# Five products per weight tile in place of six in a two-layer encoder step, with a reduction on VectorE at each evacuation

## The reference, cut to what matters

```
h = rms_norm(x, norm_ffn_w)
gate, val = split(h @ w_up)                 # 1024 -> 2 x 2816
conv = conv_b + sum_j shift(gate, j) * conv_w[j]      # width 3
x = x + (gelu(conv) * val) @ w_down         # 2816 -> 1024
```

## Time and profile before

| | |
|---|---|
| median of 3 runs | 1358.85 us (1358.19 to 1364.44) |
| span of the profiled execution | 1358.6 us |
| TensorE matmul busy | 1270.3 us, 93% |
| VectorE busy | 831.5 us, 61% |
| GpSimd busy | 688.2 us, 51% |
| ScalarE busy | 252.1 us, 19% |

### The profile page before, as it was taken

One profiled execution on the slowest core, in us unless ns is written; L12 is line 12 of the kernel. 1 busy time (PEld: TensorE's weight loads), 2 busy tenths in 40 slices (PEclk: granted clock), 3 DMA queues, 4 the chain that ended last, 5 costly groups with the idle time before them and its releaser, 6 DMA issues.

```text
span 1358.6 us, 24821 instructions
## 1 busy us (share of the span) xinstructions
PE 1270.3 (93%) x9637; PEld 1222.5 (90%) x9637; DVE 831.5 (61%) x1271; ACT 252.1 (19%) x502; POOL 688.2 (51%) x562
## 2 busy tenths in 40 slices
PE   5989999999999999999999987689999999999995
PEld 4977699999999999999999875379999999999995
DVE  7986577877778742228214556746877778772113
ACT  3023331121111210012111113523121111210000
POOL 5541155665655656665543332025755656655660
PEclk9989999999999999999999889999999999999998
DMA  5220112222222223332241110021332232222221
GB/s 200 77 86 17 33 63 94 80 90 88 82 93 80 90 78 99 99 120 80 78 126 59 52 47 32 0 73 63 94 93 78 92 93 77 93 78 93 93 77 67
DMA packets 34948, 108.91 MB, mean 80 GB/s; under 512 B 5920, under 2 KB 7728, under 8 KB 34896
## 3 DMA queue, kind: packets, MB, share of 16 engines
q1 hardware_dynamic: 28656, 102.51, 23.5%
q10 hardware_dynamic: 6240, 5.64, 1.3%
HBM read 103.00 MB, written 5.13 MB: 80 GB/s over the span
## 4 chain that ended last, share of the span: by engine, by line
PE 44%; DVE 34%; issue 13%; ACT 7%; DVEq 2%; DMA 0%; ACTq 0%; SPq 0%
PE psum L376 13%; PE psum L377 12%; PE psum L378 12%; DVE conv L1128 8%; DVE sq L1142 4%; DVE conv L1133 3%; DVE conv L1130 3%; ACT conv L779 2%; DVE gate L1081 2%; ACT y_hi L784 2%; DVE rstd L1074 1%; PE psum L504 1%; DVE sumsq L1060 1%; DVE even_winsum L1217 1%; PE psum L524 1%
## 5 line engine op out<-in xcount | busy, mean ns | idle before, releaser
L376 PE MATMUL psum<-h_hi,w_hi 128*128 128x272 f32 x2096 | 617.4, 295 | 25.6 <-DVE h_lo L1069 16.9
L378 PE MATMUL psum<-h_hi,w_lo 128*128 128x272 f32 x2096 | 611.9, 292 | 0.0
L377 PE MATMUL psum<-h_lo,w_hi 128*128 128x272 f32 x2096 | 609.0, 291 | 0.0
L354 POOL TENSOR_TENSOR w_lo<-w_raw,w_hi 128x1024 fp32r<-128x1024 f32 x187 | 461.6, 2469 | 15.6
L376 PEld LDWEIGHTS psum<-h_hi,w_hi 128*128 128x128 f32 x2096 | 400.2, 191 | 30.0 <-issue 12.6
L377 PEld LDWEIGHTS psum<-h_lo,w_hi 128*128 128x128 f32 x2096 | 401.0, 191 | 0.3
L378 PEld LDWEIGHTS psum<-h_hi,w_lo 128*128 128x128 f32 x2096 | 400.0, 191 | 0.0
L351 POOL TENSOR_TENSOR tick<-tick 1x1 f32<-1x1 f32 x183 | 36.8, 201 | 613.0 <-PE psum L378 613.0
L376 PE MATMUL psum<-y_hi,w_hi 128*128 128x272 f32 x832 | 247.1, 297 | 11.2 <-DVE y_lo L1410 4.5
L377 PE MATMUL psum<-y_lo,w_hi 128*128 128x272 f32 x832 | 245.0, 294 | 0.0
L378 PE MATMUL psum<-y_hi,w_lo 128*128 128x272 f32 x832 | 244.8, 294 | 0.0
(11 more groups left out here) (192 smaller groups left out, 1050.1 us busy)
## 6 DMA issues: line engine op xcount, KB each, us to landing
w_raw<-in_weights SPq DMA_DIRECT2D x187, 512.0 KB, 3.5
x<-in_x SPq DMA_DIRECT2D x4, 544.0 KB, 8.8
out_y<-x SPq DMA_DIRECT2D x8, 272.0 KB, 2.1
out_diff_v_new<-odd_dv ACTq DMA_DIRECT2D x1, 1024.0 KB, 4.6
out_diff_k_new<-odd_kT ACTq DMA_DIRECT2D x1, 1024.0 KB, 5.3
even_rope<-in_rope ACTq DMA_DIRECT2D x1, 544.0 KB, 9.8
odd_rope<-in_rope ACTq DMA_DIRECT2D x1, 544.0 KB, 3.7
consts<-in_consts ACTq DMA_DIRECT2D x1, 384.5 KB, 4.5
```

The costliest lines, as they stand in the source:

```text
L354: pool.tensor_tensor(w_lo[:, k], w_raw[:, k % RAW], w_hi[:, k].bitcast(F32), ALU.subtract).then_inc(w_ready, 1)
L376: pe.matmul(out, wh, xh[:, cols], start=first and n == 0, stop=False)
L377: pe.matmul(out, wh, xl[:, cols], start=False, stop=False)
L378: ins = pe.matmul(out, wl, xh[:, cols], start=False, stop=last and n == len(pairs) - 1)
```

## The change

The high and low parts of the activations are laid in one tensor with an axis for the part (`h_all`, `y_all`), at the same addresses as before. For each weight tile the 544 tokens are now cut into 240 (NB) and 304 (NA). One product of 480 columns takes the high-weight tile with the high part and the low part of the 240 tokens side by side; their two sums stay apart in PSUM. Three products of 304 columns and one of 240 do the rest. So a tile has five instructions and five weight loads in place of six, and 480 + 3x304 + 240 = 1632 columns, as before (6x272).

When a chunk is complete, VectorE first adds the two sums of the 240 tokens with a `tensor_reduce` over 240x2 elements in PSUM (`fold`, `fold_in_loop`), which writes the 240 results right ahead of the 304 others, and waits for its own result on a new semaphore `folded`; then it evacuates all 544 as one contiguous range across two banks, `whole(k)`. `grouped` reads two pieces instead of three. There is one such reduction for each output chunk: 10 and 25 in the input projections, 2x16 in the output projections, 2x44 in the up and 2x8 in the down projections, 171 in all. They are placed directly behind the wait for the slab, ahead of the evacuation.

```diff
@@ -31,6 +31,8 @@
 D, SEQ, SMP, PAST = 1024, 512, 32, 128
 T = SEQ + SMP
 HALF = T // 2
+NB = 240
+NA = T - NB
...
         x = sb("x", [P, KC, T])
         h_at = top[0]
-        h_hi = sb("h_hi", [P, KC, T], F32R)
-        h_lo_at = top[0]
-        h_lo = sb("h_lo", [P, KC, T], F32R)
+        h_all = sb("h", [P, 2, KC, T], F32R)
+        h_lo_at = h_at + KC * T * 4
+        h_hi, h_lo = h_all[:, 0], h_all[:, 1]
         y_at = top[0]
-        y_hi = sb("y_hi", [P, FC, T], F32R)
-        y_lo_at = top[0]
-        y_lo = sb("y_lo", [P, FC, T], F32R)
+        y_all = sb("y", [P, 2, FC, T], F32R)
+        y_lo_at = y_at + FC * T * 4
+        y_hi, y_lo = y_all[:, 0], y_all[:, 1]
...
@@ -207,11 +209,24 @@
 
             return psum[:, 2 * k:2 * k + 2, 0:HALF]
 
+        banks = psum[:, :, :].rearrange("p b n -> p (b n)")
+
+        def whole(k):
+
+            return banks[:, 1024 * (k + 1) - T:1024 * (k + 1)]
+
+        def beside(k):
+
+            return psum[:, 2 * k, 0:2 * NB].rearrange("p (z n) -> p n z", z=2)
+
+        def together(k):
+
+            return whole(k)[:, 0:NB]
+
         def pieces(k):
 
-            return [(psum[:, 2 * k, 0:HALF], 0, HALF),
-                    (psum[:, 2 * k + 1, 0:SEQ - HALF], HALF, SEQ - HALF),
-                    (psum[:, 2 * k + 1, SEQ - HALF:HALF], SEQ, SMP)]
+            v = whole(k)
+            return [(v[:, 0:SEQ], 0, SEQ), (v[:, SEQ:T], SEQ, SMP)]
...
@@ -367,19 +383,21 @@
         def _(pe):
             def tiles(acc, s, pairs, first, last):
 
-                for n, (kt, xh, xl) in enumerate(pairs):
+                a, b = psum[:, 2 * acc + 1, 512 - NA:512], psum[:, 2 * acc, 0:NB]
+                both = psum[:, 2 * acc, 0:2 * NB].rearrange("p (z n) -> p z n", z=2)
+                for n, (kt, z) in enumerate(pairs):
                     wh = w_hi[:, s % RING, kt * P:(kt + 1) * P]
                     wl = w_lo[:, s % RING, kt * P:(kt + 1) * P]
-                    for half in range(2):
-                        cols = slice(half * HALF, (half + 1) * HALF)
-                        out = psum[:, 2 * acc + half, 0:HALF]
-                        pe.matmul(out, wh, xh[:, cols], start=first and n == 0, stop=False)
-                        pe.matmul(out, wh, xl[:, cols], start=False, stop=False)
-                        ins = pe.matmul(out, wl, xh[:, cols], start=False, stop=last and n == len(pairs) - 1)
+                    begin, end = first and n == 0, last and n == len(pairs) - 1
+                    pe.matmul(both, wh, z[:, :, 0:NB], start=begin, stop=False)
+                    pe.matmul(a, wh, z[:, 0, NB:T], start=begin, stop=False)
+                    pe.matmul(a, wh, z[:, 1, NB:T], start=False, stop=False)
+                    pe.matmul(a, wl, z[:, 0, NB:T], start=False, stop=end)
+                    ins = pe.matmul(b, wl, z[:, 0, 0:NB], start=False, stop=end)
                 return ins
...
@@ -1069,6 +1087,14 @@
                 ve.scalar_tensor_tensor(h_lo[:, ch], x[:, ch], w, h_hi[:, ch].bitcast(F32),
                                         ALU.mult, ALU.subtract).then_inc(h_ready, 1)
 
+            folds = [0]
+
+            def fold(acc):
+
+                ve.tensor_reduce(together(acc), beside(acc), AX.X, ALU.add).then_inc(folded, 1)
+                folds[0] += 1
+                ve.wait_ge(folded, folds[0])
...
@@ -1084,7 +1110,8 @@
             def add_out(slab, value, acc, m):
 
                 ve.wait_ge(slab, value)
-                ve.tensor_tensor(halves(x[:, m]), halves(x[:, m]), pair(acc), ALU.add).then_inc(x_upd, 1)
+                fold(acc)
+                ve.tensor_tensor(x[:, m], x[:, m], whole(acc), ALU.add).then_inc(x_upd, 1)
...
             def ffn(layer, n_norm, upd0):
                 s0, d0, f0 = S_UP[layer], S_DOWN[layer], FC * layer
 
+                fold0 = folds[0]
+
+                def fold_in_loop(before, acc):
+
+                    ve.tensor_reduce(together(acc), beside(acc), AX.X, ALU.add).then_inc(folded, 1)
+                    ve.wait_ge(folded, before + 1)
...
@@ -1116,6 +1150,7 @@
                     if layer or not (isinstance(i, int) and i == 0):
                         ve.wait_ge(conv_ready, 2 * i + (f0 + p - 1))
                     settle(ve)
+                    fold_in_loop(4 * i + (fold0 + 2 * p), 2 * p)
                     grouped(g, 2 * p, 2).then_inc(gate_out, 1)
...
@@ -1135,7 +1170,8 @@
                     ve.wait_ge(slab_done, 4 * i + (s0 + 2 * p + 2))
                     if layer or not (isinstance(i, int) and i == 0):
                         ve.wait_ge(y_ready, 2 * i + (f0 + p - 1))
-                    ve.tensor_tensor(halves(sq[:, p]), pair(2 * p + 1), halves(rstd), ALU.mult).then_inc(val_out, 1)
+                    fold_in_loop(4 * i + (fold0 + 2 * p + 1), 2 * p + 1)
+                    ve.tensor_tensor(sq[:, p], whole(2 * p + 1), rstd[:, :], ALU.mult).then_inc(val_out, 1)
...
@@ -1161,12 +1197,13 @@
                 with ve.Fori(0, 2) as i:
                     for j in range(4):
                         ve.wait_ge(slab_done, 12 * i + (d0 + 3 * j + 3))
-                        ve.tensor_tensor(halves(x[:, 4 * i + j]), halves(x[:, 4 * i + j]), pair(j % 2),
-                                         ALU.add).then_inc(x_upd, 1)
+                        fold_in_loop(4 * i + (fold0 + UP + j), j % 2)
+                        ve.tensor_tensor(x[:, 4 * i + j], x[:, 4 * i + j], whole(j % 2), ALU.add).then_inc(x_upd, 1)
                         if n_norm < 3:
                             norm_low(j, n_norm + 1, i)
                         ve.wait_ge(sum_add, 4 * i + (KC * (n_norm + 1) + j))
                         add_square(j, n_norm + 1, i)
+                folds[0] += UP + KC
...
```

More of the change, by code:

```diff
@@ L405, in in_projection, with out_chunk @@
                     side(n)
-            def out_chunk(s, m, acc, yh, yl, c0):
+            def out_chunk(s, m, acc, z, c0):
                 pe.wait_ge(w_ready, s + 1)
-                part = [(4 * (m % 2) + c, yh[:, c0 + c], yl[:, c0 + c]) for c in range(4)]
+                part = [(4 * (m % 2) + c, z[:, :, c0 + c]) for c in range(4)]
                 tiles(acc, s, part, True, True).then_inc(slab_done if m % 2 else mid_done, 1)
@@ L452, in down @@
                                 pe.wait_ge(y_ready, f0 + f + 1)
-                            ins = tiles(j % 2, d0 + k, [(f - lo, y_hi[:, f], y_lo[:, f])], f == 0, f == FC - 1)
+                            ins = tiles(j % 2, d0 + k, [(f - lo, y_all[:, :, f])], f == 0, f == FC - 1)
                         ins.then_inc(slab_done, 1)
@@ L1194, in rotate @@
             def rotate(acc, z, swapped, rope, kT, qT_dst):
-                o(ve.stream_shuffle(halves(swapped), pair(acc), PARTNER))
-                o(ve.tensor_tensor(halves(z), pair(acc), halves(rope[:, 0]), ALU.mult), evac)
+                o(ve.stream_shuffle(swapped, whole(acc), PARTNER))
+                o(ve.tensor_tensor(z, whole(acc), rope[:, 0], ALU.mult), evac)
                 o.wait()
@@ L1247, in _ @@
                 elif n == 3:
-                    o(ve.tensor_tensor(halves(e_vT), pair(acc), halves(rstd), ALU.mult), evac)
+                    o(ve.tensor_tensor(e_vT[:, :], whole(acc), rstd[:, :], ALU.mult), evac)
                     scale_rope(e_rope)
@@ L1333, in _ @@
                 acc = 2 + n % 2
-                src = pair(acc)
+                src = whole(acc)
                 ve.wait_ge(slab_done, S_ODD_IN + n + 1)
+                fold(acc)
                 if kind == "cr":
-                    o(ve.tensor_tensor(halves(o_cr[0:16, :]), src[0:16], halves(rstd[0:16, :]), ALU.mult), evac)
+                    o(ve.tensor_tensor(o_cr[0:16, :], src[0:16], rstd[0:16, :], ALU.mult), evac)
                 elif kind == "cq":
-                    o(ve.scalar_tensor_tensor(halves(o_q[:, n - 1]), src, 0.125, halves(rstd), ALU.mult, ALU.mult), evac)
+                    o(ve.scalar_tensor_tensor(o_q[:, n - 1], src, 0.125, rstd[:, :], ALU.mult, ALU.mult), evac)
                 elif kind == "ck":
-                    o(ve.tensor_tensor(halves(o_k[:, n - 3]), src, halves(rstd), ALU.mult), evac)
+                    o(ve.tensor_tensor(o_k[:, n - 3], src, rstd[:, :], ALU.mult), evac)
                 elif kind == "cg":
-                    o(ve.tensor_tensor(halves(o_sg[:, n - 13]), src, halves(rstd), ALU.mult), evac)
+                    o(ve.tensor_tensor(o_sg[:, n - 13], src, rstd[:, :], ALU.mult), evac)
                 elif n < 17:
@@ L1346, in _ @@
                         ve.wait_ge(turned, n - 5)
-                    o(ve.tensor_tensor(halves(oz[:, n % 2]), src, halves(rstd), ALU.mult), evac)
+                    o(ve.tensor_tensor(oz[:, n % 2], src, rstd[:, :], ALU.mult), evac)
                 if n == 5:
```

9 lines of the change are left out of this document (5 added, 4 removed).

## The result

The changed kernel took 1373.49 us, median of 4 runs (1370.10 to 1377.05), beside 1360.01 for the kernel before; the ratio is 1.0090, 95% interval 1.0066 to 1.0113. It is slower by 0.9%, 13.5 us. The forecast was 1358 us. The time lies in the wide range over the rivals (1324 to 1382) and on the side that had the largest chance, but outside the forecast's own 1350 to 1369.

What follows compares the result with a forecast made beforehand. TensorE was taken to bound most of the time, VectorE a few stages. From the profiled 1358.6 us, -16.9 for products and +16.4 for late reductions gave 1358.1, forecast as 1358 us; own range 1350 to 1369, over the rivals 1324 to 1382.

Steps and rivals of the forecast that it cites:

- the wide range over the rivals: Whole time: 1324 to 1382 us, reaching to the two rivals on columns with their bounds, leaving out short product and VectorE.
- the side that had the largest chance: Whole time: slower had chance 0.42, against same 0.30 and faster 0.28.
- The price of a product: Dense stretches: 12.8 ns are a cost per instruction, so a tile goes from 756.6 to 744.0 ns.
- the two rivals that put the loss on columns: Tiles: loss per column, 757 ns, 1373 us, chance 0.17; or from reading weights and tokens together, 727 ns, chance 0.17.
- The rival of the short product: Tiles: the 240-column product is slow, a tile takes over 1000 ns; chance 0.12.
- The sum of the products: TensorE-bound tiles, 1338 of 1464: 12.6 ns saved each, 16.9 us; bounds nothing and 40 us.
- The reductions: VectorE: 171 at 0.69 us each with wait, mostly hidden in feed-forward parts; 16.4 us late in all, 7 to 30.
- its rival: Up projections: VectorE becomes the bound, a chunk takes 13.2 us in place of 11.9, 1406 us and more; chance 0.08.
- L1128's counterpart still over 2 us long: Up projection: sign that VectorE still waits for GpSimd; if short and TensorE waits for `gate_out`, VectorE bounds.
- odd input projection: TensorE's three waits for `att_masked`, behind a reduction each: 2.0 us late; its last slab 0.7.
- part of it taken from waits for GpSimd; I take 2.5 each: Second halves of the output projections: reductions delay TensorE's wait for `x_upd`, at most 5.5 us each, 5.0 taken together.
- fillings with one accumulator, and the odd attention's chain: 3.0: Attention stages: reductions in these fillings and in the odd attention's chain come late by 3.0 us.

Runs made afterwards that it cites:

- run 1: Changed kernel without its reductions, the five products per tile kept and one high-weight, low-part product left out of the sums: 1349.32 us, 0.9914 of the kernel before.
- run 2: Kernel before, six products per tile kept, with the 171 reductions and their waits added at the same places: 1384.08 us, ratio 1.0177.
- run 5: Changed kernel with VectorE making the last low parts of the odd attention before the last sum of the first half: 1369.26 us, 1.0064 of the kernel before.
- run 11: Changed kernel with 17 unread fp32 products on TensorE ahead of its wait before the second half of the odd output projection: 1368.17 us.
- run 4: Changed kernel with five products and reductions only in the projections around attention, six products in the feed-forward parts: 1379.01 us, 1.0136 of the kernel before.

## Why the prediction was right or wrong

**The price of a product** was right where it was read. The tile came out at 743 ns against 744.0, and the two rivals that put the loss on columns, 757 and 727 ns, are refuted by it. There is luck in how near it came: the 480-column product costs 4 ns more than forecast and the 240-column one 4 less, and in other executions the same tile takes 750. No run shows the terms of the forecast's sum, 12.8 ns for each product and 680 ns for the 1632 columns; the traces show whole distances. In their place stands a stretch of the kernel before at a granted clock of 0.50:

```profile
778.12:782.43 4.31, 4.31 (x21) 4.31 (x21) 0.75 (x1) 0.31 (x1) 0.00 (x0) 0.50 0.16 66
...
778.12 0.43 PE L377 MATMUL psum<-h_lo,w_hi 128*128 128x272 f32 x1
...
782.43 0.43 PE L378 MATMUL psum<-h_hi,w_lo 128*128 128x272 f32 x1
```

4.31 us for 19 distances are 226.8 ns each, 1.20 columns per ns. Twice that rate for a granted clock of 1.00, which is an estimate, leaves 12.7 of the 126.1 ns; by it the surplus after 480, 304 and 240 columns is 17, 12 and 9 ns, so an even 12.8 does not hold. (The trace gives the stretch of the earlier trace rows a granted clock of 1.00 and not a lower one, though its products stand 227.1 ns apart; why is not shown.) A tile with one product fewer saved 13.3 or 6.7 ns. **The rival of the short product**, a tile of over 1000 ns, is refuted at 240 columns, but with 192 a tile does lose (780 ns against 743 to 750), not by the short product itself (89 ns, 0.46 a column) but mostly in the product behind it.

**The sum of the products** was mis-sized: 16.9 us forecast, 11.2 measured by run 1 (8 to 15 by its interval). The step that failed is the multiplication of one price by 1338 tiles. A price read in one stretch of the up projection was carried to stretches whose tile took 750 ns, and around attention hardly anything arrives at all: the six stages outside the feed-forward part together gained 0.8 us in run 1, where (1338-1056) x 12.6 ns = 3.6 were counted.

**The reductions** cost 659 to 661 ns each, 0.69 with their wait as assumed. That the 88 in the up projections are hidden was right, to 0.00 us in run 2, and the 16 in the down projections did not lengthen their stages. VectorE did not become the bound, its rival falls. One of the forecast's signs was wrong: it wanted L1128's counterpart still over 2 us long, or else VectorE as the bound. It takes 605 ns and TensorE is gapless, since the wait had moved to the copy ahead of it; and as the reductions take time that VectorE had spent in such waits, its share rose to 63% and not to the forecast's 70%. The cost of the rest was mis-sized: 16.4 us forecast, 23.5 measured by run 2, of which its trace shows 20.4. By its stages, forecast and found:

```
                                       forecast   run 2
even input projection                    3.0       2.0
even output projection, second half      2.5       1.7
odd output projection, second half       2.5       7.2
odd input projection                     2.7       5.7
attention stages with their fillings     3.0       3.4
ends of up, and down projections         2.0      -1.5
start and end of the span                0.7       1.9
```

(The first row's terms, 3 x 0.6 + 0.7 + 0.6, make 3.1. The two input projections are within what changes between executions of the same instructions, as said above.)

The step that failed, and that the runs show, is "part of it taken from waits for GpSimd; I take 2.5 each": the odd second half cost 7.2 us in run 2 and 6.4 in the changed kernel. The forecast let a later VectorE meet only waits, which a delay shortens. It can as well be pushed from beside a short step of GpSimd's, which it waits out in 0.7 us, into a long one; then 0.7 us become 2.4. And it left TensorE's clock out of the price of a wait: the lost 2.4 us became 4.9, since the idle engine came back at a granted clock of 0.50; it was 1.00 without the wait (run 5) and with products in it (run 11). The even second half has no such collision and came out below its forecast. The same omission of the clock bears on "fillings with one accumulator, and the odd attention's chain: 3.0": in the changed kernel the odd attention with its fillings cost 6.7 us and the even one -1.0, with a granted clock of 0.81 in the stretch shown above. That the clock falls there is measured; what makes it fall stays open.

The odd input projection shows the same pattern ahead of its sixth slab. TensorE's wait for the evacuation of `k`, in the kernel before and then in the changed one:

```profile
PE psum L376 <- DVE odd_gla_k L1341: 0.4, 1, 0.4
```

```profile
PE psum L392 <- DVE odd_gla_k L1380: 2.8, 1, 2.8
```

That is 2.4 us more, with reductions of 0.7 us each in front; in runs 2, 4, 5 and 11, which have the same reductions, it is 1.6 us, so 1.2 more. I argue the cause from the rows and tested it by no run. In the later slabs of this stage the stretches at a granted clock of 0.50 lie in other slabs in each kernel: 752.5 to 759.0, 776.5 to 782.5 and 797.0 to 803.0 us before, 735.5 to 742.0, 759.5 to 765.5 and 783.0 to 786.0 us after (against the kernel before, the changed one has a slab that is 4.1 us longer and, six slabs on, one that is 2.9 us shorter), so that neither the size of this stage's loss nor its causes are shown.

**The whole**: -11.2 + 23.5 = +12.3 us by parts, +13.5 measured. The forecast had -16.9 + 16.4. The errors, 5.7 us in the first and 7.1 in the second, have the same sign; either alone would have left the time within 0.5% of the kernel before.

## What to carry to other kernels

Work added to an engine costs by place, not by duration: 103 of the 171 reductions here lengthened no stage (all those of the feed-forward parts but the very last), and one place with a reduction in front lost 4.9 us. Ask of each place where a delay would push the instructions behind it, whether a long step of GpSimd lies there (here 2.46 us in place of 0.73 for one subtraction), and how long the engine that waits in the end will stand idle (here 2.44 us lost to a granted clock of 0.50 behind 3.9 us of idleness). Change a stage at a time: the same change, kept out of the stages where TensorE waits for VectorE, turned 0.9% lost into 0.5 to 0.8% gained. When a saving is some nanoseconds per instruction, read the price in every stage in which it is to be multiplied, and in more than one execution. And before a stage's length in one trace is taken for an effect, look how far it changes between kernels that have the same instructions there.

## What the runs showed of the hardware

- The same gapless stream of five products runs at 743.3 or at 750.0 ns a tile, and holds either through hundreds of tiles. Both occur in one execution of one kernel (262.68 and 264.98 us for the two up projections of run 5) and for the same program in two executions (262.76 in the changed kernel and 264.97 us in run 11 for the first). The down projections show both too (16.50 and 16.35 us for a column of 22 tiles, in the changed kernel and in run 11). One or three empty instructions ahead of the stream changed nothing. Six products of 272 columns kept to 756.7 in every run. What chooses is open.
- At a granted clock of 1.00 and 743 ns a tile the distance is 109 ns after 240 columns, 139 after 304 and 217 after 480 (at 750 ns a tile: 111, 139 and 223), 0.45 to 0.46 ns a column, but 200, 0.52 a column, after 384 columns behind a product of 192.
- Products of 272 columns stood 226.8 ns apart at a granted clock of 0.50 (kernel before, 778.12 to 782.43 us) and 126.1 at 1.00.
- A subtraction of 128 columns on VectorE took 0.29 us alone, 0.73 beside a step on GpSimd that ended 0.59 us after its start, and 2.46 beside one that began 0.02 us ahead of it and took 2.34.
- After 3.9 us of idleness TensorE ran a chunk of four tiles at a granted clock of 0.50; with products of no use in that wait it ran the same chunk at 1.00, and the chunk was 2.44 us shorter.
